# First expert's gather ahead of the sums, last four rows gathered in halves

## What is computed

```python
q = (xc @ w_q).reshape(TOKEN_CHUNK, PEER_HEADS, 2, PEER_HALF)
s = jnp.einsum('thpd,pkd->thpk', q, sub_keys)
sv, si = lax.top_k(s, PEER_TOPK)                      # 16 best of 128 keys, on each of two sides
cand = sv[:, :, 0, :, None] + sv[:, :, 1, None, :]    # 256 sums of pairs
cand_id = si[:, :, 0, :, None] * PEER_NKEYS + si[:, :, 1, None, :]
cv, ci = lax.top_k(cand.reshape(..., 256), PEER_TOPK) # 16 best sums
eid = take_along_axis(cand_id.reshape(..., 256), ci)  # their experts, of 16384
g = jax.nn.softmax(cv, axis=-1)
act = jax.nn.gelu(jnp.einsum('thkd,td->thk', u[eid], xc))
y = jnp.einsum('thk,thkd->td', g * act, v[eid])
```

## Time and profile before

| | |
|---|---|
| median of 3 runs | 1575.68 us (1574.5 to 1578.08) |
| the profiled execution's own time | 1575.04 us |
| its span (first to last instruction) | 1573.3 us |
| mean granted TensorE clock | 0.937 of full speed |
| busy: PE, DVE, ACT, POOL | 82%, 73%, 58%, 42% |
| moved | 643.51 MB, mean 409 GB/s; 536.90 MB of it by gathers |
| chain that ended last, by engine | DMA 43%, PE 26%, DVE 18%, ACT 6% |

### The profile page before, as it was taken

One profiled execution on the slowest core, in us unless ns is written; L12 is line 12 of the kernel. 1 busy time (PEld: TensorE's weight loads), 2 busy tenths in 40 slices (PEclk: granted clock), 3 DMA queues, 4 the chain that ended last, 5 costly groups with the idle time before them and its releaser, 6 DMA issues.

```text
span 1573.3 us, 18796 instructions
## 1 busy us (share of the span) xinstructions
PE 1284.6 (82%) x5582; PEld 788.0 (50%) x5582; DVE 1149.6 (73%) x2692; ACT 914.3 (58%) x3307; POOL 662.0 (42%) x516
## 2 busy tenths in 40 slices
PE   8999898886898788766688978797778888787875
PEld 8986566543554556533355546564445542222321
DVE  2159998877888869636778887976778777777545
ACT  2236566557667546434676664655676666666676
POOL 0014344455445333223554433335554445554552
PEclk9999999997999899986899989999999999999999
DMA  9979999999999999999999999999999999999997
GB/s 393 397 320 401 408 413 420 421 421 422 402 389 408 421 420 421 421 421 419 421 417 410 396 417 422 419 420 421 421 418 416 396 410 421 421 421 421 421 420 292
DMA packets 89742, 643.51 MB, mean 409 GB/s; under 512 B 9976, under 2 KB 10536, under 8 KB 11816
## 3 DMA queue, kind: packets, MB, share of 16 engines
q0 software_dynamic: 73728, 536.90, 82.8%
q1 hardware_dynamic: 15588, 105.18, 16.2%
q10 hardware_dynamic: 324, 0.23, 0.0%
HBM read 641.23 MB, written 1.05 MB: 408 GB/s over the span
## 4 chain that ended last, share of the span: by engine, by line
DMA 43%; PE 26%; DVE 18%; ACT 6%; issue 5%; POOL 2%; SPq 0%; DVEq 0%; POOLq 0%; ACTq 0%
DMA ring<-in_uv,expert 41%; PE ybank L675 13%; PE bank L476 9%; DVE ring L1181 7%; DVE xs L1194 2%; POOL ring L1316 2%; DMA wring<-in_chunks 2%; PE bank L622 1%; ACT wgt L885 1%; ACT diag L895 1%; PE bank L611 1%; ACT th L883 1%; DVE buf L974 1%; DVE picked L977 1%; DVE si L930 1%
## 5 line engine op out<-in xcount | busy, mean ns | idle before, releaser
L1316 POOL DMA_INDIRECT ring<-in_uv,expert x512 | 661.8, 1293 | 890.8 <-PE ybank L675 546.2
L675 PE MATMUL ybank<-ring,diag 128*128 128x512 f32 x1528 | 790.7, 653 | 260.7 <-ACT diag L895 259.8
L1181 DVE SCALAR_TENSOR_TENSOR ring<-ring,tok 128x1024 f32<-128x1024 f32 x512 | 624.4, 1224 | 311.3 <-DMA ring<-in_uv,expert 305.8
L675 PEld LDWEIGHTS ybank<-ring,diag 128*128 128x128 f32 x1528 | 282.4, 200 | 654.6 <-ACT diag L895 417.7
L877 ACT ACTIVATE sq<-dots 128x1 f32<-128x1 f32 x512 | 102.8, 201 | 512.2 <-DVE ring L1181 511.2
L885 ACT ACTIVATE wgt<-th,half_p 128x1 f32<-128x1 f32 x512 | 198.1, 387 | 17.1
L476 PEld LDWEIGHTS bank<-hT,wring 128*128 128x128 f32 x1536 | 186.0, 199 | 35.1 <-issue 31.0
L476 PE MATMUL bank<-hT,wring 128*128 128x128 f32 x1536 | 186.8, 282 | 8.4 <-DMA wring<-in_chunks 8.1
L1194 DVE SCALAR_TENSOR_TENSOR xs<-ring,wgt,xs 128x1024 f32<-128x1024 f32 x128 | 164.0, 1282 | 5.2 <-ACT wgt L885 3.7
L895 ACT ACTIVATE diag<-cst,wgt 128x128 f32<-128x128 f32 x382 | 153.4, 402 | 15.9 <-PE ybank L675 3.6
L883 ACT ACTIVATE th<-arg,dots 128x1 f32<-128x1 f32 x512 | 150.8, 295 | 16.6
(11 more groups left out here) (126 smaller groups left out, 791.8 us busy)
## 6 DMA issues: line engine op xcount, KB each, us to landing
wring<-in_chunks SPq DMA_DIRECT2D x52, 1024.0 KB, 9.6
held<-in_chunks SPq DMA_DIRECT2D x24, 1024.0 KB, 24.8
ring<-in_chunks SPq DMA_DIRECT2D x20, 1024.0 KB, 12.0
ring<-in_uv,expert POOLq DMA_INDIRECT x512, 11.9
xs<-in_x SPq DMA_DIRECT2D x2, 512.0 KB, 4.3
wpool<-in_w_pool SPq DMA_DIRECT2D x2, 512.0 KB, 13.4
trunk_out<-buf SPq DMA_DIRECT2D x4, 256.0 KB, 4.8
ring<-in_pool_scale SPq DMA_DIRECT2D x1, 512.0 KB, 14.3
```

What stands on the lines that cost most here:

```text
L675: ins = pe.matmul(ybank[m][:, :], diag[:, nth % DIAGS, :], ring[:, (2 * t + r) % RING, D + m * BANK:D + (m + 1) * BANK], start=(nth == ten ...
L1181: dve.scalar_tensor_tensor(out=ring[:, g % RING, 0:D], in0=ring[:, g % RING, 0:D], scalar=1.0, in1=tok[:, :], op0=ALU.mult, op1=ALU.mult, ...
L1316: pool.indirect_dma_start(ring[:, g % RING, :], None, uv, bass.IndirectOffsetOnAxis(ap=expert[:, at:at + 1], axis=0)).then_inc(row_landed[ ...
```

## The change

At the head, as soon as the best key of each side is known, the number of the first expert is worked out from these two (the best sum is that of the two best keys) and published alone; gather 0 waits only for that, gathers 1 to 7 for the rest of the eight, which `experts(0, 1, 7)` writes later. All counts of `expert_ready` move up by one.

At the end, the last four rows (508 to 511, `HALVED = 4`) are gathered as eight transfers of 4 KB per token: the four u halves, with index 2 x expert, then the four v halves, with index 2 x expert + 1. The indices are made beside those of the last head. The v halves have semaphores of their own. TensorE adds columns 0 to 511 of these four rows, DVE columns 512 to 1023 (one addition of 512 columns per row, `close_last`). The last tick is no longer a case of its own in `rows_on_tensor`.

The final norm of tile 1 is split accordingly: ACT squares the DVE half from SBUF first, then the TensorE half straight from the PSUM bank, each with a sum; DVE combines the two sums. ACT scales columns 512 to 1023, DVE scales columns 0 to 511 from PSUM with the root and the gain in one operation; the gain of these columns was copied to SBUF in tile 0's final part. Tile 1's outputs are sent in the order of their readiness, columns 0 to 511 on `normed_v`, then 512 to 1023 on `normed_a`.

```diff
--- before.py
+++ after.py
@@ -73,6 +73,8 @@
 DMA_SCRATCH = 2048
 OUTS = 4
 
+HALVED = 4
+
 REACH = max(WINDOWS)
 
 C_ID = 0
@@ -176,12 +178,16 @@
         cv = sb("cv", [P, TOPK])
         ci = sb("ci", [P, TOPK], U32)
         cab = sb("cab", [P, 2, TOPK], U32)
+        best = sb("best", [P, 2])
         cabf = sb("cabf", [P, 2, TOPK])
         picked = sb("picked", [P, 2, TOPK])
         cmax = sb("cmax", [P, 1])
         gsum = sb("gsum", [P, 1])
         prob = sb("prob", [P, HK])
         expert = sb("expert", [P, HK], U32)
+
+        last_halves = sb("last_halves", [P, 2, HALVED], U32)
+        half_ssq = sb("half_ssq", [P, 1])
 
         buf1 = sb("buf1", [P, 2 * D])
         gates = buf1[:, :]
@@ -315,8 +322,6 @@
 
         def rows_on_tensor(t):
 
-            if t == windows * TICKS - 1:
-                return ()
             return (1,) if t in shared else (0, 1)
 
         def rows_on_vector(t):
@@ -324,7 +329,9 @@
 
         def experts_of(w, h):
 
-            return PH * w + h + 2
+            return PH * w + h + 3
+
+        halved_from = windows * HK - HALVED
 
         def tensor_rows(t):
 
@@ -671,11 +678,14 @@
                 return
             nth = tensor_rows(t) + rows_on_tensor(t).index(r)
             pe.wait_ge(diag_done, nth + 1)
-            for m in range(2):
+            halved = 2 * t + r >= halved_from
+            if halved:
+                pe.wait_ge(last_v_landed[2 * t + r - halved_from], 16)
+            for m in range(1 if halved else 2):
+                rows_here = tensor_rows((w + 1) * TICKS) - (HALVED if last and m else 0)
                 ins = pe.matmul(ybank[m][:, :], diag[:, nth % DIAGS, :],
                                 ring[:, (2 * t + r) % RING, D + m * BANK:D + (m + 1) * BANK],
-                                start=(nth == tensor_rows(w * TICKS)),
-                                stop=(nth == tensor_rows((w + 1) * TICKS) - 1))
+                                start=(nth == tensor_rows(w * TICKS)), stop=(nth == rows_here - 1))
             ins.then_inc(pe_summed, 1)
 
         def scalar_mix(act, w):
@@ -982,6 +992,11 @@
                 step(dve.scalar_tensor_tensor(out=picked[:, 0, these], in0=picked[:, 0, these], scalar=float(NK),
                                               in1=picked[:, 1, these], op0=ALU.mult, op1=ALU.add))
                 settle(dve)
+                if w == windows - 1 and h == PH - 1:
+                    for side in range(2):
+                        step(dve.tensor_scalar(last_halves[:, side, :], picked[:, 0, TOPK - HALVED:TOPK], 2.0,
+                                               float(2 * layer * EXPERTS + side), ALU.mult, ALU.add))
+                    settle(dve)
                 dve.tensor_scalar(expert[:, h * TOPK + lo:h * TOPK + lo + n], picked[:, 0, these],
                                   float(layer * EXPERTS), None, ALU.add).then_inc(expert_ready, 1)
 
@@ -994,6 +1009,11 @@
                 for r in range(2):
                     dve.wait_ge(*read(w, f"score0{'ab'[r]}"))
                     key_search(0, (r,))
+
+                step(dve.tensor_copy(best[:, :], si[:, :, 0]))
+                settle(dve)
+                dve.scalar_tensor_tensor(out=expert[:, 0:1], in0=best[:, 0:1], scalar=float(NK),
+                                         in1=best[:, 1:2], op0=ALU.mult, op1=ALU.add).then_inc(expert_ready, 1)
                 sums = tmp[:, 0:64]
                 square = sums.rearrange("p (i j) -> p i j", i=8)
                 all_sums(square, 8)
@@ -1001,7 +1021,7 @@
                 places(8, 3)
                 for a in range(2):
                     pick_side(a, 0, 8, square)
-                experts(0, 0, 8)
+                experts(0, 1, 7)
 
             def weigh_heads(h):
                 mine = prob[:, h * TOPK:(h + 1) * TOPK]
@@ -1203,23 +1223,22 @@
 
         def close_last(dve):
 
-            t = windows * TICKS - 1
-            dve.wait_ge(pe_summed, tensor_rows(t))
-            for r in range(2):
-                g = 2 * t + r
-                dve.wait_ge(wgt_done, vector_rows(t) + r + 1)
-                if r:
+            before = tensor_rows(halved_from // 2)
+            part = x_of(NT - 1)[:, BANK:D]
+            dve.wait_ge(pe_summed, before)
+            for i in range(HALVED):
+                g = halved_from + i
+                dve.wait_ge(diag_done, before + i + 1)
+                dve.wait_ge(last_v_landed[i], 16)
+                if i:
                     settle(dve)
-                for m in range(2):
-                    part = x_of((windows - 1) % NT)[:, m * BANK:(m + 1) * BANK]
-                    ins = dve.scalar_tensor_tensor(
-                        out=part, in0=ring[:, g % RING, D + m * BANK:D + (m + 1) * BANK],
-                        scalar=wgt[:, g % COLS:g % COLS + 1], in1=part if r else ybank[m][:, :],
-                        op0=ALU.mult, op1=ALU.add)
-                    if r:
-                        ins.then_inc(x_final, 1)
-                    else:
-                        step(ins)
+                ins = dve.scalar_tensor_tensor(out=part, in0=ring[:, g % RING, D + BANK:2 * D],
+                                               scalar=wgt[:, g % COLS:g % COLS + 1],
+                                               in1=part if i else ybank[1][:, :], op0=ALU.mult, op1=ALU.add)
+                if i == HALVED - 1:
+                    ins.then_inc(x_final, 1)
+                else:
+                    step(ins)
 
         def vector_row(dve, t, r):
             w, n = t // TICKS, t % TICKS
@@ -1232,34 +1251,66 @@
...
+            step(dve.tensor_copy(last_gain, filled_bank(dve, windows, "final0")[:, :]))
...
+        all_summed = tensor_rows(windows * TICKS)
+
+        last_gain = gates[:, D:D + BANK]
+
+        def last_scalar(act):
+            act.activation(warm[:, 2:3], gelu_bias[:, :], ACT.Sqrt)
+            act.wait_ge(x_final, 2 * windows - 1)
+            act.activation(gates[:, BANK:D], x_of(1)[:, BANK:D], ACT.Square,
+                           accum_out=stat[:, 1, 0:1]).then_inc(ssq_done, 1)
+            act.wait_ge(pe_summed, all_summed)
+            act.activation(gates[:, 0:BANK], ybank[0][:, :], ACT.Square, accum_out=half_ssq[:, 0:1]
+                           ).then_inc(ssq_done, 1)
+            act.wait_ge(rinv_done, 2 * windows + 2)
+            act.activation(stat[:, 1, 2:3], stat[:, 1, 1:2], ACT.Sqrt).then_inc(root_done, 1)
+            act.wait_ge(root_done, 2 * windows + 2)
+            act.wait_ge(gained, 3)
+            act.activation(normed(1)[:, BANK:D], normed(1)[:, BANK:D], ACT.Copy,
+                           scale=stat[:, 1, 2:3]).then_inc(normed_a, 1)
+
+        def last_vector(dve):
+            dve.wait_ge(x_final, 2 * windows - 1)
+            dve.tensor_tensor(normed(1)[:, BANK:D], x_of(1)[:, BANK:D],
+                              filled_bank(dve, windows, "final1")[:, :], ALU.mult).then_inc(gained, 1)
+            mean = stat[:, 1, 1:2]
+            dve.wait_ge(ssq_done, 2 * windows + 2)
+            step(dve.tensor_scalar(mean, stat[:, 1, 0:1], 1.0 / D, EPS, ALU.mult, ALU.add))
+            settle(dve)
+            dve.wait_ge(ssq_done, 2 * windows + 3)
+            step(dve.scalar_tensor_tensor(out=mean, in0=half_ssq[:, 0:1], scalar=1.0 / D, in1=mean,
+                                          op0=ALU.mult, op1=ALU.add))
+            settle(dve)
+            dve.reciprocal(mean, mean).then_inc(rinv_done, 1)
+            dve.wait_ge(root_done, 2 * windows + 2)
+            dve.scalar_tensor_tensor(out=normed(1)[:, 0:BANK], in0=ybank[0][:, :], scalar=stat[:, 1, 2:3],
+                                     in1=last_gain, op0=ALU.mult, op1=ALU.mult).then_inc(normed_v, 1)
@@ -1278,29 +1329,26 @@
...
                 close_last(dve)
-                for _ in final_vector(dve, 1):
-                    pass
+                last_vector(dve)
 
             @block.gpsimd
             def _(pool):
+                half_rows = uv.rearrange("n (h d) -> (n h) d", h=2)
                 for g in range(windows * HK):
                     w, at = g // HK, g % HK
-                    if g == 0:
-                        pool.wait_ge(expert_ready, 1)
-                    elif g == 8:
-                        pool.wait_ge(expert_ready, 2)
+                    if g in (0, 1, 8):
+                        pool.wait_ge(expert_ready, (0, 1, 8).index(g) + 1)
                     elif at % TOPK == 0:
                         pool.wait_ge(expert_ready, experts_of(w, at // TOPK))
                     if g == 0:
@@ -1313,10 +1361,22 @@
                             pool.wait_ge(pe_summed, tensor_rows(t) + rows_on_tensor(t).index(r) + 1)
                         else:
                             pool.wait_ge(dve_summed, vector_rows(t) + rows_on_vector(t).index(r) + 1)
+                    if g < halved_from:
+                        pool.indirect_dma_start(
+                            ring[:, g % RING, :], None, uv,
```

(68 more changed lines are left out.)

## The result

| | before | after |
|---|---|---|
| median of 4 runs | 1576.37 us | 1555.68 us (1554.21 to 1558.59) |
| ratio | | 0.9873, 95% interval 0.9859 to 0.9887 |
| the profiled execution's own time, span | 1575.04, 1573.3 us | 1556.39, 1554.6 us |
| bytes moved | 643.51 MB | 643.51 MB |
| mean rate over the span | 409 GB/s | 414 GB/s |

The account below looks back on a forecast made before the run. The byte stream was taken to set the pace mostly, with DVE the bound at the head and serial work at the tail. Head 0.55 plus tail 2.55 gave 3.1 us, so 1575.68 became 1572.6, range 1570.5 to 1575.2.

Parts of the forecast that it names:

- takes 2.49 us of the stream: Whole gather stream: one gathered row of 1.05 MB at 421 GB/s takes 2.49 us.
- rival 3: Last four rows: stream pays per gather or packet, not per byte; 9.6 us lost, 1582.2 in all; chance 0.06.
- The tail: Serial work after the last byte, plus the halved last rows and split norm: 2.55 us gained, bounds 0.8 to 2.9.
- The Sqrt table's load: Final norm on ScalarE: the load begins at about the time the last half lands; 1.50 us from load to square.
- ACT's diag of the last row: End of ScalarE's chain for row 511: ends at 1563.08, with the last v half landing at 1563.7.
- ACT's two squares: Final norm: two half squares of 0.72 us each, from 1564.6 to 1566.05.
- Packets: Tail gathers: four more gathers put 32 more packets on each engine, at 10 ns a packet 0.33 us.
- Rival 2: Tail: slow GpSimd gathers bring the last v halves 1.8 us late; tail gains 0.8, 1574.4 in all; chance 0.20.
- The head's 0.55: Start of the stream: an earlier first gather removes DVE's waits before the third and fourth dots, 0.55 us gained.
- The added work: Head, on DVE: one small copy and one small multiply-add delay all that follows by 0.28 us.
- Rival 1: Head: the whole 2.2 us of lead survives, 1.65 more gained, 1570.9 in all; chance 0.13.
- a stream below 356 GB/s in 190 to 204 us: Sign for the head: a stream below that rate, or sooner starved, says the lead was spent.

Follow-up runs that it names:

- b3: Kernel before with the ring at 168192 and only the tail's part (last four rows in halves, shared sums, split norm): 1556.75 us, ratio 0.9877.
- a4: Whole change with 8 unused floats ahead of the ring, putting it at 168224, 32 past a multiple of 256: 1577.07 us, ratio 1.0010.
- b2: Kernel before with the ring at 168192 and only the head's part (first expert gathered ahead of the sums): 1557.99 us, ratio 0.9890.
- b1: Kernel before with the ring at 168192 and neither part of the change: 1559.00 us, ratio 0.9889.
- c3: Kernel before with the weight chunks (held, wring) moved to a multiple of 256, ring left 160 past one: 1572.86 us, ratio 0.9982.

## Why the prediction was wrong

- **The step that failed** is the first one: a row of 1.05 MB "takes 2.49 us of the stream". I took 421 GB/s for a property of the transfers and carried it through the changed kernel. It was the rate at that ring address; at 168192 it is 427, 2.46 us a row. In one row the difference is 0.035 us, in 512 rows 18 us; 16.5 us were measured with the address alone.
- **The edit that I did not price** is three lines of the diff that issue no instruction: the declarations of `best`, `last_halves` and `half_ssq`. The part by part account left them out. No rival covered the rate of the stream as a whole either; rival 3 had it going the other way, in 4 of 512 rows.
- **The tail was right**: 2.55 forecast, 2.25 by the medians of b3, and in the trace 3.7 us from the last landing to the last scaling where 3.8 was forecast. The Sqrt table's load began 0.4 before the last half landed, as forecast. ACT's diag of the last row ended at 1547.23, 0.4 before that landing; my count, made for the row's time of 2.49, had 0.6. ACT's two squares took 1.28 to the end of the second read (1548.65 to 1549.93), against 1.45. Packets: v halves landed 1.24 to 1.25 apart (DVE's starts at 1546.42 and 1547.66), against 1.23 by the full rate, so 32 more packets an engine cost 0.1 to 0.2 us by this estimate, not 0.33. Rival 2 did not happen: the v gathers took 0.93 each, not 1.93. Rival 3 did not either.
- **The head's 0.55 is of the right size at the dot of row 3, but out of two wrong terms.** The added work delayed DVE's first dot by 0.72 and not by 0.28. The waits for landings that it removes in 110 to 260 us were 0.8 in the one trace I had, the lowest of nine; the others have 1.0 to 2.7, and of the five traces with the head's part only a4 keeps one (1.0). The two errors pull against each other, which is luck: 0.8 us in the mean at the dot of row 3, 0.0 to 1.3 in single traces. Rival 1 asked for 2.2 and is in no trace at that dot. Its sign, a stream below 356 GB/s in 190 to 204 us if the lead was spent, tells nothing: it is 347 in b2 with the head's part and 347 in b1 without.
- Of the 20.7 us, then, 16.5 are the ring's address, 2.5 the two parts together by the medians (3.1 by the means of eight, as forecast); the remaining 1.7 are the spread of the medians: the kernel before stood 0.9 higher beside the first runs (1576.37 against 1575.5), the changed one 0.8 lower (1555.68 against 1556.47).

## What to carry to other kernels

Before a change to a kernel that streams at its transfer limit is credited or blamed, compare the rate in a full stretch before and after: if it moved, look at the addresses of the destinations, which a few bytes of new tiles shift. Keep every large transfer's destination at a multiple of 256 bytes in its partition, and measure a change's parts with that address held fixed. An earlier start of a stream is worth only the waits that the bounding engine has for it, less the work that it adds there. Read such a wait from several executions: here it was 0.8 us in one and 2.7 in another.

## What the runs showed of the hardware

A destination off the grain of 256 bytes costs 8 KB packets 1.4% of the stream (421 against 427 GB/s), for GpSimd's gathers and, by the single run c3, for SyncE's loads too. Five offsets cost nearly the same, which I had not expected. The Trainium skill (DMA: Bandwidth & Descriptors, "How a descriptor splits into AXI transactions") says that a transaction must start at a multiple of 256 bytes and that a descriptor that does not start there fetches the bytes before its start for nothing. Its 256 bytes are the grain of the runs, though the page speaks of what a transaction reads, and the runs moved the side that is written. The price does not: counted by its beats it would grow from 1 in 257 at 32 past to 7 in 263 at 224 past, an estimate of 0.4% to 2.7%, while 32 past ran at 420 GB/s and 224 past at 420; and counted by its transactions, 33 instead of 32, it would be 3%, twice what was measured. Which side's transactions make the difference was not tried: all runs moved the destination in SBUF and left the source in HBM alone. The section on the chip, above, has the DMA engines move data to PSUM too. No trace shows that: every transfer listed for the kernel before and the changed one goes to or from a tile in SBUF.
